# Two-block transformer kernel on one core: layer one's expert steps 256 to 512, with layer two's modulation moved into the first part of the routing, and its norm, queries and values set beside the last routing pass

## The chip, the cores and the metric

The kernel runs on one core of a Trainium2 chip. The metric is the device time of one execution, in microseconds (us), as the median of several runs. A core has TensorE (PE in the profile, with its weight loads as PEld), VectorE (DVE), ScalarE (ACT), GpSimd (POOL) and SyncE (SP). Here POOL only issues the gathers of expert rows, and SP only issues the loads of weights; both kinds of transfer run on the same 16 DMA engines.

## What is computed

Two different transformer blocks, one after the other, all in float32 on 256 tokens of width 1024. The first block has two layers and carries a context of another 256 tokens along, which layer two reads only for its keys and values. Each layer has a modulation (scales and shifts computed from a conditioning vector), attention with two softmax maps, two side branches, and a feed-forward part that is a memory of 16384 experts:

```python
for l in range(2):                                   # first block
    mod = (silu(c) @ w_mod[l] + b_mod[l]).reshape(b, 6, 1, d)   # 12 column blocks of 512
    xn = modulate(rms_norm(h, norm1_g[l]), mod[:, 0], mod[:, 1])
    p = xn @ w_in[l]                                 # queries, keys, values, pool, conv, gates
    q, k = rope(qk_heads(p[.., Q], q_norm_g[l])), rope(qk_heads(p[.., K], k_norm_g[l]))
    o = diff_attn(q, [k, k_context], [v, v_context])
    h = h + mod[:, 2] * mixer_output(o, p, ...)
    h = h + mod[:, 5] * peer_ffn(modulate(rms_norm(h, norm2_g[l]), ...), ...)
    # the context rows go through the same steps in layer one

def peer_ffn(x, w_q, sub_keys, u_emb, v_emb):        # per token
    s = scores of 8 heads x 2 halves against 128 sub-keys
    eidx, gate = top-16 of the sums of two top-16 lists, per head  # the "routing": 128 experts
    hid = gelu(x . u_emb[eidx])
    return sum_k(gate_k * hid_k * v_emb[eidx_k])
```

The second block (two layers of SwiGLU, retention, block attention and convolution) follows and is not touched.

## The kernel before

Tokens are held in blocks of 128, one token per partition. Layer one works on four of them: A0 and A1 (the sequence) and B2 and B3 (the context). The expert part of one block is 128 *steps*. In step s POOL gathers, for each of the 128 tokens, the row of its next expert (u and v side by side, 8 KB a token, so 1 MiB a gather); DVE multiplies the u half by the token and sums (L1717), ACT and DVE form the weight, ACT makes a diagonal matrix of it (L1131), and PE adds the v half into an accumulator through that diagonal (L698, two matmuls a row, printed as four; pairs of rows at a time, `V_LAG` = 3 steps behind). In blocks A1 and B3, which the code calls `SHARED`, PE does only one row in four this way, and DVE does the other three (L1710).

The steps of A0, A1, B2, B3 are numbered 0 to 511 and run without a break. Beside them each engine runs other work, written as generators that `yield` a number of *beats*; `weave(..., 2)` lets two beats of other work pass for each expert step. All three engines run the same sequence of yields (ACT and DVE two beats later than PE), so the place of every piece of other work in the steps is fixed by these numbers. From step 256 on the other work is `pe_ahead`, `act_ahead` and `dve_ahead`:

- the routing of B2's heads 2 to 7 in three passes of two heads, then that of B3 in one pass of eight heads (`pe_route_scores`, L674, and `dve_route_pass`). A pass of two heads has 46 yields which weigh 50 beats, times 0.62 by `scaled`; the pass of eight has 136 yields which weigh 161 beats, times 0.85;
- layer two's modulation (`pe_modulation`, L479 and L469): 12 column blocks, each with two weight tiles of 1 MiB. `together(a, b, rate)` gives one item of `a`, at no beats of its own, for `rate` yields of `b`;
- `pe_tokens`, times 0.8: layer two's first norm for the sequence (`pe_norm_turn`, L455), its queries (column blocks n = 0, 1), keys (2, 3) and values (4, 5) (`pe_qkv_heads`; L429, eight matmuls printed as sixteen for each n and block of tokens; `dve_qkv_heads` normalises the heads of queries and keys and rotates them), and then its mixer (`pe_mixer`: pool, conv and gate branches).

After step 511 comes the edge "hand over", where layer two goes on with the context's keys and values.

Weights come into a ring of four tiles of 1 MiB (`W`, slots of `wbuf`) in the order in which `sync` issues them; a tile is loaded as soon as the one that held its slot has been used, so the ring always holds the next four. Gathers go into a ring of ten slots (`gat`), from which `gat.held` leaves some out while their memory has another use: two of ten are left out up to gather 340 and three after it. A slot comes free when PE (or DVE) has used the v half of its row. The heads of queries and keys pass through the ring `side`, which lies in the memory that the routing also uses (`sc`), and partly in that of the routing's queries.

## Time and profile before

| | before |
|---|---|
| median of 3 runs | 4387.02 us (4383.78 to 4387.35) |
| profiled execution, its own time | 4379.6 us |
| its span, first to last instruction | 4377.8 us |
| PE / PEld busy | 3754.2 / 2394.2 us |
| DVE busy | 2843.8 us |
| ACT busy | 1153.1 us |
| DMA, mean over the span | 280 GB/s |

The rows come from one profiled execution. Busy time is a union per engine; the end of a matmul is modelled. "DMA share" in a stretch is the busy share of the 16 DMA engines. Arrows (`<-`) name what ended an idle time. The stretch in question runs from about 1509 us to 2371 us of the span.

### The profile page before, as it was taken

The numbers are of one execution on the slowest core, as the hardware profiler recorded it, in microseconds if no ns is written. First come the engines' busy times: TensorE is split into PE (matmuls) and PEld (weight loads), VectorE is DVE, ScalarE is ACT, GpSimd is POOL, SyncE is SP. The second block draws the span as 40 slices with busy tenths as digits, with TensorE's granted clock in tenths as the row PEclk, the third lists the DMA queues.
The fourth block names the chain that finished last, engine by engine and source line by source line (L and its number), as shares of the span: only waits on it lengthen the run. The fifth ranks groups of instructions, "written<-read, shape, count | busy, mean of one in ns | idle before, by whom it ended". The sixth has DMA issues, their size and how long they took to land. (4 is left out here: it accounts for less than half of the span.)

```text
span 4377.8 us, 42320 instructions
## 1 busy us (share of the span) xinstructions
PE 3754.2 (86%) x15261; PEld 2394.2 (55%) x15261; DVE 2843.8 (65%) x6607; ACT 1153.1 (26%) x2555; POOL 901.2 (21%) x772
## 2 busy tenths in 40 slices
PE   6989978788999787789896878777779989999898
PEld 3457444334746333245642544322229879998797
DVE  1441147988876777877877548886666576565765
ACT  2140011124011111131011411112114444444443
POOL 0000012433332333423332014544330000000000
PEclk7999989999999899999997989999999999999999
DMA  7114358987999999979996149999984534545343
GB/s 294 77 41 161 149 203 344 408 344 302 420 416 363 389 418 421 394 303 382 421 421 275 74 179 389 421 383 422 422 365 167 178 129 158 199 157 183 136 164 130
DMA packets 246622, 1225.90 MB, mean 280 GB/s; under 512 B 19256, under 2 KB 46202, under 8 KB 124428
## 3 DMA queue, kind: packets, MB, share of 16 engines
q0 software_dynamic: 110592, 805.36, 45.2%
q1 hardware_dynamic: 135820, 417.84, 25.5%
q8 instruction: 120, 1.97, 0.2%
q14 instruction: 90, 0.74, 0.0%
HBM read 1222.07 MB, written 1.05 MB: 279 GB/s over the span
## 5 line engine op out<-in xcount | busy, mean ns | idle before, releaser
L429 PE MATMUL ps<-wbuf,BIG 128*128 128x512 f32 x1856 | 812.0, 595 | 7.9 <-DMA wbuf<-in_t_conv_out_w 4.1
L2554 POOL DMA_INDIRECT gbuf<-in_t_uv,idx x286 | 336.5, 1176 | 1493.6 <-DVE BIG L1682 860.2
L429 PEld LDWEIGHTS ps<-wbuf,BIG 128*128 128x128 f32 x1856 | 352.0, 191 | 440.8 <-issue 431.6
L1758 DVE TENSOR_TENSOR plo<-wbuf,phi 128x1024 fp32r<-128x1024 f32 (+1 forms) x344 | 401.7, 1180 | 285.9 <-ACT phi L1166 285.2
L698 PE MATMUL ps<-gbuf,BIG 128*128 128x512 f32 x868 | 435.2, 641 | 150.9 <-ACT BIG L1131 144.3
L698 PE MATMUL ps<-BIG 128*128 128x512 f32 x904 | 438.8, 625 | 126.7 <-ACT BIG L1131 124.9
L1146 ACT ACTIVATE BIG<-BIG 128x2 f32<-128x2 f32 x384 | 78.1, 203 | 1480.1 <-DVE BIG L1724 1480.0
L1717 DVE CUSTOM_DVE_ANT_0 BIG<-BIG 128x1024 f32<-128x1024 f32 x292 | 355.9, 1222 | 156.2 <-DMA BIG<-in_t_uv,idx 155.2
L723 PE MATMUL ps<-XH,phi 128*128 128x256 f32 x1472 | 422.8, 287 | 24.9 <-DVE XL L1768 21.0
L2554 POOL DMA_INDIRECT BIG<-in_t_uv,idx x292 | 336.9, 1154 | 428.5 <-PE ps L698 362.7
L1717 DVE CUSTOM_DVE_ANT_0 gbuf<-gbuf,BIG 128x1024 f32<-128x1024 f32 x286 | 348.9, 1222 | 116.1 <-DMA gbuf<-in_t_uv,idx 115.2
L724 PE MATMUL ps<-XL,phi 128*128 128x256 f32 x1472 | 421.2, 286 | 0.0
L725 PE MATMUL ps<-XH,plo 128*128 128x256 f32 x1472 | 421.1, 286 | 0.0
L429 PE MATMUL ps<-BIG,wbuf 128*128 128x256 f32 x1920 | 420.4, 379 | 0.3 <-DMA wbuf<-in_t_conv 0.3
L1166 ACT CAST phi<-wbuf 128x1024 fp32r<-128x1024 f32 (+1 forms) x344 | 343.8, 1013 | 291.6 <-PE ps L725 291.0
L429 PEld LDWEIGHTS ps<-BIG,wbuf 128*128 128x128 f32 x1920 | 364.9, 190 | 63.4 <-issue 14.0
L698 PE MATMUL ps<-wbuf,BIG 128*128 128x512 f32 x604 | 312.2, 649 | 97.2 <-ACT BIG L1131 97.2
L698 PEld LDWEIGHTS ps<-BIG 128*128 128x128 f32 x904 | 173.7, 199 | 377.5 <-issue 197.5
L698 PEld LDWEIGHTS ps<-gbuf,BIG 128*128 128x128 f32 x868 | 166.3, 202 | 385.5 <-ACT BIG L1131 215.6
L2554 POOL DMA_INDIRECT wbuf<-in_t_uv,idx x190 | 227.6, 1198 | 432.2 <-PE ps L698 399.7
L723 PEld LDWEIGHTS ps<-XH,phi 128*128 128x128 f32 x1472 | 286.3, 194 | 26.8 <-DVE XL L1768 22.3
L1131 ACT ACTIVATE BIG<-ident,BIG 128x128 f32<-128x128 f32 x594 | 210.3, 395 | 296.9 <-DVE BIG L1700 279.5
(348 smaller groups left out, 5086.6 us busy)
## 6 DMA issues: line engine op xcount, KB each, us to landing
wbuf<-in_t_in SPq DMA_DIRECT2D x84, 1024.0 KB, 8.3
wbuf<-in_t_w_mod SPq DMA_DIRECT2D x48, 1024.0 KB, 9.3
wbuf<-in_ffn_wg SPq DMA_DIRECT2D x20, 2048.0 KB, 7.6
wbuf<-in_ffn_wu SPq DMA_DIRECT2D x20, 2048.0 KB, 7.7
wbuf<-in_t_conv SPq DMA_DIRECT2D x48, 768.0 KB, 8.6
wbuf<-in_ffn_wd SPq DMA_DIRECT2D x16, 2048.0 KB, 7.9
wbuf<-in_t_peer_wq SPq DMA_DIRECT2D x24, 1024.0 KB, 6.9
wbuf<-in_w_in SPq DMA_DIRECT2D x14, 1536.0 KB, 6.6
```

The costliest lines, as they stand in the source:

```text
L429: ins = p(mm)(bank, l, r, start=(k == 0), stop=(k == 7))
L698: ins = p(mm)(ps.of(("acc", T, tb, n)), dg, g[:, 1024 + n * 512:1536 + n * 512], start=(j == 0), stop=(j == last_on_pe(T, tb)))
L723: p(mm)(bank, lh, rh, start=(start and i == 0), stop=False)
L724: p(mm)(bank, lh, rl, start=False, stop=False)
L725: ins = p(mm)(bank, ll, rh, start=False, stop=(stop and i == n - 1))
L1131: a(act)(dg, ident[:, :], ACT.Copy, scale=wv[:, j:j + 1]).then_inc(act_exp.up(T, tb, "diag", j), 1)
L1146: a(act)(x2[:, j - 1:j + 1], x2[:, j - 1:j + 1], ACT.Tanh, scale=GELU_C * GELU_K).then_inc(act_exp.up(T, tb, "tanh", j // 2), 1)
L1166: a(copy)(piece_at(q)[0], W2.of(key, rows_, n)[:, k0:k1, c0:c1]).then_inc(act_piece.up(q), 1)
L1717: v(ttr)(row, row, XN[:, tb, :], 1.0, 0.0, ALU.mult, ALU.add, hid[:, j:j + 1]).then_inc(dve_exp.up(T, tb, "u", j), 1)
L1758: v(tt)(lo, W2.of(key, rows_, n)[:, k0:k1, c0:c1], hi.bitcast(F32), ALU.subtract).then_inc(dve_piece.up(q), 1)
L2554: g(nc.gpsimd.indirect_dma_start)(slot, None, I["t_uv"], bass.IndirectOffsetOnAxis(ap=idx[:, tb % 3, j:j + 1], axis=0)).then_inc(g_landed[ ...
```

## The change

In `*_ahead` of all three engines: the modulation is put beside the routing of B2's heads 2 to 7 alone, at one column block for 9 yields where it was 18. Then the one routing pass of B3 begins (one yield), and a new `alongside` sets the norm, the queries and the values (n = 0, 1, 4, 5) of layer two beside it: one beat of the tokens' work pulls 2.4 yields of the routing, and only the routing's beats count. Behind it come the keys (n = 2, 3) and the mixer as before, at 0.8. The heads go through a new ring `heads` (eight slots in the memory of the routing's queries) in place of `side`; ACT and DVE wait for the modulation before the norm; the third gather slot is left out from gather 300 and not 340; SP issues the weights in the new order.

```diff
+def alongside(a, b, rate):
+    m = 0
+    for n in a:
+        m += rate * (n or 1)
+        while m >= 1:
+            m -= 1
+            n = next(b, None)
+            if n is not None:
+                yield n
+    yield from b
...
+        heads = Ring([BIG[:, 8192 + i * 512:8704 + i * 512] for i in range(8)])
...
-        heads_ring = {"A": wide, "B": side, "C": side, "D": wide}
+        heads_ring = {"A": wide, "B": side, "C": heads, "D": wide}
...
         def pe_ahead(p):
             yield
-            routes = both(*(scaled(pe_route_scores(p, "B", "A", 2, h, h + 2), 0.62, 1) for h in (2, 4, 6)),
-                          scaled(pe_route_scores(p, "B", "A", 3), 0.85, 1))
-            yield from together(pe_modulation(p, 1), routes, 18)
-            yield from scaled(pe_tokens(p), 0.8, 1)
+            routes = both(*(scaled(pe_route_scores(p, "B", "A", 2, h, h + 2), 0.62, 1) for h in (2, 4, 6)))
+            yield from together(pe_modulation(p, 1), routes, 9)
+            routes = scaled(pe_route_scores(p, "B", "A", 3), 0.85, 1)
+            yield next(routes)
+            yield from alongside(pe_tokens(p), routes, 2.4)
+            yield from scaled(pe_keys(p), 0.8, 1)
...
             yield from pe_norm_turn(p, "C1", range(2))
-            yield from pe_qkv_heads(p, "C", "C1", 0, L, range(6), range(2))
+            yield from pe_qkv_heads(p, "C", "C1", 0, L, (0, 1, 4, 5), range(2))
+
+        def pe_keys(p):
+            L = second
+            yield from pe_qkv_heads(p, "C", "C1", 0, L, (2, 3), range(2))
             edge(p, ("attended", "C"))
             yield from pe_mixer(p, "C", 1, L)
...
         def act_tokens(a):
             L = second
             edge(a, "tokens")
+            a.wait_ge(*dve_mod.at(1, "A", 1))
...
         def dve_tokens(v):
             L = second
             edge(v, "tokens")
-            side.reset(*edges.events("tokens"))
+            v.wait_ge(*dve_mod.now())
+            heads.reset(*edges.events("tokens"))
...
-                if s == 340:
+                if s == 300:
                     gat.held = {7, 8, 9}
...
-            sync_qkv(s, "C", 1, 0, range(6))
+            sync_qkv(s, "C", 1, 0, (0, 1, 4, 5, 2, 3))
```

What it does to the order on the engines is seen at three places.

On PE, in the routing of B2's heads: the modulation's column blocks (L479 before, L493 after; `32x512 x8`) stand among the rows of the experts' v halves (L698 before, L712 after; two a row). Before, from the third block on:

```order
L479 MATMUL ps<-wbuf,BIG 32x512 x8
L469 MATMUL ps<-BIG 128x2 x4
L698 MATMUL ps<-gbuf,BIG 128x512 x2
L698 MATMUL ps<-wbuf,BIG 128x512 x2
L674 MATMUL ps<-BIG 128x128 x4
L698 MATMUL ps<-wbuf,BIG 128x512 x2
L698 MATMUL ps<-BIG 128x512 x6
L479 MATMUL ps<-wbuf,BIG 32x512 x8
```

After:

```order
L493 MATMUL ps<-wbuf,BIG 32x512 x8
L483 MATMUL ps<-BIG 128x2 x4
L712 MATMUL ps<-wbuf,BIG 128x512 x2
L712 MATMUL ps<-BIG 128x512 x6
L493 MATMUL ps<-wbuf,BIG 32x512 x8
L483 MATMUL ps<-BIG 128x2 x4
L712 MATMUL ps<-gbuf,BIG 128x512 x4
L493 MATMUL ps<-wbuf,BIG 32x512 x8
```

Between two column blocks there were six expert rows (twelve matmuls), and there are now two or four.

On PE, where the routing of B3 is done and layer two's norm (L455), first queries (L429) and their turn (L422) follow, before:

```order
L455 MATMUL ps<-BIG,H 128x128 x12
L429 MATMUL ps<-wbuf,BIG 128x512 x8
L698 MATMUL ps<-BIG 128x512 x2
L698 MATMUL ps<-gbuf,BIG 128x512 x6
L429 MATMUL ps<-wbuf,BIG 128x512 x8
L698 MATMUL ps<-wbuf,BIG 128x512 x4
L698 MATMUL ps<-BIG 128x512 x4
L429 MATMUL ps<-wbuf,BIG 128x512 x8
L422 MATMUL ps<-ident,sc 128x128 x4
```

After, the same work begins right behind B3's scores (L688; norm L469, queries L443):

```order
L688 MATMUL ps<-BIG 128x128 x16
L712 MATMUL ps<-wbuf,BIG 128x512 x2
L712 MATMUL ps<-BIG 128x512 x2
L469 MATMUL ps<-BIG,H 128x128 x4
...
L469 MATMUL ps<-BIG,H 128x128 x8
L712 MATMUL ps<-wbuf,BIG 128x512 x4
L443 MATMUL ps<-wbuf,BIG 128x512 x8
L712 MATMUL ps<-BIG 128x512 x4
L712 MATMUL ps<-gbuf,BIG 128x512 x6
L712 MATMUL ps<-wbuf,BIG 128x512 x4
L712 MATMUL ps<-BIG 128x512 x2
L443 MATMUL ps<-wbuf,BIG 128x512 x8
```

Between two blocks of queries there were four expert rows, and there are now eight.

On POOL, the gathers of one turn of the ring at about gather 310, before:

```order
L2554 DMA wbuf<-in_t_uv,idx 128x2048 x2
L2554 DMA BIG<-in_t_uv,idx 128x2048 x3
L2554 DMA gbuf<-in_t_uv,idx 128x2048 x3
```

After:

```order
L2588 DMA wbuf<-in_t_uv,idx 128x2048 x2
L2588 DMA BIG<-in_t_uv,idx 128x2048 x2
L2588 DMA gbuf<-in_t_uv,idx 128x2048 x3
```

One turn had eight slots there and has seven, as it had from gather 340 on before.

## Rows read from the trace of the kernel before

**Rows 1.** The page's part 2: the span in 40 slices of 109 us.
```profile
PEclk7999989999999899999997989999999999999999
DMA  7114358987999999979996149999984534545343
GB/s 294 77 41 161 149 203 344 408 344 302 420 416 363 389 418 421 394 303 382 421 421 275 74 179 389 421 383 422 422 365 167 178 129 158 199 157 183 136 164 130
```

**Rows 2.** Windows: stretch, length, busy us (xinstructions) by engine, clock, DMA share, GB/s.
```profile
1509.00:1663.60 154.60, 121.38 (x400) 51.73 (x401) 115.84 (x375) 27.44 (x85) 51.69 (x44) 0.89 0.98 405
1663.60:1775.00 111.40, 86.57 (x276) 37.92 (x275) 75.57 (x270) 20.10 (x63) 39.57 (x36) 0.91 1.01 421
1775.00:1869.30 94.30, 64.72 (x135) 24.95 (x133) 89.13 (x243) 16.78 (x56) 40.68 (x33) 0.96 0.97 381
1869.30:1882.00 12.70, 10.36 (x41) 6.92 (x42) 4.67 (x18) 4.75 (x10) 1.88 (x2) 0.73 0.55 189
1882.00:1934.00 52.00, 52.00 (x130) 23.44 (x129) 33.70 (x82) 17.54 (x36) 13.63 (x13) 1.00 0.79 304
1934.00:1983.00 49.00, 38.88 (x97) 17.78 (x96) 41.44 (x82) 18.59 (x32) 12.94 (x12) 0.90 0.82 329
1983.00:2050.00 67.00, 63.81 (x159) 28.60 (x157) 53.81 (x108) 12.35 (x30) 25.43 (x18) 1.00 0.98 390
2050.00:2313.00 263.00, 238.53 (x752) 145.25 (x753) 213.94 (x422) 26.63 (x85) 94.97 (x76) 0.97 1.01 418
2313.00:2371.00 58.00, 27.48 (x49) 10.11 (x48) 46.74 (x89) 3.90 (x14) 21.73 (x17) 0.75 0.99 403
```

**Rows 3.** DMA view of 1509 to 2371 us.
```profile
DMA packets 47939, 339.22 MB, mean 394 GB/s; under 512 B 5594, under 2 KB 5734, under 8 KB 8294
q0 software_dynamic: 36352, 264.70, 75.6%
q1 hardware_dynamic: 11548, 74.07, 20.9%
```

**Rows 4.** Timeline of PE: start us, us, instruction, count, idle before.
```profile
1508.89 3.46 PE L479 MATMUL ps<-wbuf,BIG 128*32 128x512 f32 x16 [6.41 <-DVE BIG L1306]
...
1653.32 1.92 PE L479 MATMUL ps<-wbuf,BIG 128*32 128x512 f32 x16
...
1663.61 3.73 PE L674 MATMUL ps<-BIG 128*128 128x128 f32 x32
...
1871.21 2.04 PE L455 MATMUL ps<-BIG,H 128*128 128x128 f32 x8 [3.42 <-DVE BIG L1358]
...
1881.95 7.03 PE L429 MATMUL ps<-wbuf,BIG 128*128 128x512 f32 x16
1888.82 1.88 PE L698 MATMUL ps<-BIG 128*128 128x512 f32 x4
...
1934.33 1.04 PE L422 MATMUL ps<-ident,modd 128*128 128x128 f32 x8
```

**Rows 5.** DMA view of 1676 to 1753 us: issues, median us to landing.
```profile
BIG<-in_t_uv,idx POOLq DMA_INDIRECT x11, 17.4
```

**Rows 6.** The same view, 1780 to 1862 us.
```profile
BIG<-in_t_uv,idx POOLq DMA_INDIRECT x8, 9.5
```

**Rows 7.** Timeline of DVE: the first block of queries.
```profile
1893.44 0.69 DVE L1433 TENSOR_REDUCE st<-sc 128x8 f32<-128x512 f32 x1 [5.42 <-ACT sc L982]
...
1894.89 0.20 DVE L1437 RECIPROCAL st<-st 128x8 f32<-128x8 f32 x1 [0.56 <-ACT st L925]
...
1898.19 0.69 DVE L1412 TENSOR_TENSOR sc<-sc,rope 128x512 f32<-128x512 f32 x1
...
1899.52 0.42 DVE L1417 TENSOR_TENSOR sc<-sc,BIG 128x256 f32<-128x256 f32 x1
```

**Rows 8.** Waits of DVE, 1869.3 to 1983 us: us in total, times, longest.
```profile
DVE st L1433 <- ACT sc L982: 12.2, 3, 5.6
DVE BIG L1358 <- PE ps L455: 6.9, 1, 6.9
```

More of the change, by code:

```diff
@@ L2396, in act_tokens, with act_keys @@
             edge(a, "tokens")
+            a.wait_ge(*dve_mod.at(1, "A", 1))
             yield from act_norm_turn(a, "C1", L, range(2), colA(1, 0), colB(1, 0))
-            yield from act_qkv_heads(a, "C", "C1", 1, 0, L, range(6), range(2), side)
+            yield from act_qkv_heads(a, "C", "C1", 1, 0, L, (0, 1, 4, 5), range(2), heads)
+        def act_keys(a):
+            L = second
+            yield from act_qkv_heads(a, "C", "C1", 1, 0, L, (2, 3), range(2), heads)
             edge(a, ("attended", "C"))
@@ L2515, in dve_tokens, with dve_keys @@
             edge(v, "tokens")
-            side.reset(*edges.events("tokens"))
+            v.wait_ge(*dve_mod.now())
+            heads.reset(*edges.events("tokens"))
             yield from dve_norm_turn(v, "C1", L, range(2), colA(1, 0), colB(1, 0), "A experts", sideb)
-            yield from dve_qkv_heads(v, "C", "C1", 1, 0, L, range(6), range(2), side)
+            yield from dve_qkv_heads(v, "C", "C1", 1, 0, L, (0, 1, 4, 5), range(2), heads)
+        def dve_keys(v):
+            L = second
+            yield from dve_qkv_heads(v, "C", "C1", 1, 0, L, (2, 3), range(2), heads)
             edge(v, ("attended", "C"))
@@ L2708, in restart @@
             last.clear()
-            for ring in (ps, gat, diag, mrows, big, tmp, wide, side, side4, narrow, sideb, sts):
+            for ring in (ps, gat, diag, mrows, big, tmp, wide, side, side4, heads, narrow, sideb, sts):
                 ring.reset()
```

20 lines of the change are left out of this document (12 added, 8 removed).

## Prediction

> **What bounds the kernel now.** I read first the page's slices. From the seventh to the twenty-first the DMA line is near full [rows 1]: while experts run, transfers set the pace, and the stretch that the change touches (slices 14 to 22) runs at 382 to 421 GB/s with one dip, to 303, in the eighteenth slice, before it ends in the last of them. Second, I cut this stretch by its content. Markers on PE give the cuts [rows 4]: the modulation's first column block at 1508.9 us, its eighth at 1653.3; B3's scores (L674 x32) at 1663.6; the norm at 1871.2; the first queries at 1882.0; the turn of the gate columns (L422 on modd) at 1934.3, which stands at the border from B2's rows to B3's. The code's yields agree: three passes at 31 beats are 46.5 steps, and the window from 1509.0 to 1663.6 us has 44 gathers; 161 times 0.85 beats are 68.5 steps, and the next two windows have 69 [rows 2].
>
> Third, the price of a byte. At 421 GB/s one MiB takes 2.49 us. The first window moved 405 GB/s times 154.6 us, which is 59.7 MiB: its 44 gathers and 16 weight tiles. So time there is bytes. Over the whole stretch the two queues moved 339 MB, which is three quarters gathers [rows 3], and the change moves the same bytes. What it can win is only the time in which the DMA engines were short of work. I take it per window as its length times (1 - GB/s / 421) [rows 2]: 5.9 us to 1663.6; 0 and 9.0 us in B3's routing; 7.0 in the norm; 14.5 to 1934; 10.7 to 1983; 4.9 to 2050; 1.9 to 2313; 2.5 at the end. Together 56 us, of which 32 lie between 1869 and 1983 us.
>
> Why there? From 1882 to 1934 PE is busy 52.00 of 52.00 us. A block of queries or keys takes PE 7.03 us and an expert row up to 1.88 us [rows 4]; the plan puts 3.2 steps between two blocks, so a turn costs 7 + 3.2 times 1.8, about 13 us, while its 4.2 MiB need 10.5 us. That is a stretch bound by PE. In the 94.3 us before, DVE is busy 89.13 us [rows 2]: the second half of the routing is bound by DVE. And in the window before that one neither is full (DVE 75.57 and PE 86.57 of 111.4 us), because weights fill the DMA engines. The change puts PE's work from the third kind of place beside DVE's work of the other two.
>
> **Part one, modulation beside B2's heads 2 to 7.** At 9 yields a block, 138 yields take all twelve blocks. In the window the ring then loads 24 tiles and not 16: 8 MiB more, +19.9 us. DVE needs 115.84 us and PE 121.38 us (at a granted clock of 0.89) of some 174 us, and eight gather slots are still there up to gather 300, with landings of 17.4 us at worst when weights compete [rows 5]; one turn of that ring would be 8 times 3.9 us. So I add no wait: between 0 and +5 us (waits of PE for a weight tile, which this stretch does not show at L479), taken as 0.
>
> **Part two, norm, queries and values beside B3's routing.** This stretch took 205.7 us for 79 MiB. Its tiles are still eight (the last four of modulation and the first of the queries before; values and keys after), so its floor by bytes stays 205.7 - 9.0 = 196.7 us. DVE had 164.7 us of work. Four blocks of queries add 4.6 us each: five operations of 0.69 us, for which L1433 and L1412 stand, two of 0.42 and two small ones [rows 7]; the norm adds at most the 4.67 us of its window. That makes 188 us. PE has 69 rows at up to 1.88, eight blocks at 6.9 (1881.95 to 1888.82), B3's scores at 3.7 and the norm at under 5, at most 194 us. So three engines stand at 96 to 98% of 197 us at once. Something gives way. Two places show how far it goes. In 1775 to 1869, with seven slots, DVE reached 94.5% and DMA 0.97; in 1983 to 2050 PE reached 95% with DMA at 0.98. DVE's 188 us at 94.5% are 199 us. On top come its waits in its own order: the heads wait for ACT's square, which waits behind PE's block, and the second diagonal of the norm waits for PE [rows 8]. Half of the 12.2 us (four of eight blocks) and the norm's 6.9 us make 13, of which I take 12, since the blocks stand eight steps apart. 211 us, +5.3 us. The bounds: 197 (nothing collides) and 232 (a wait of 5.6 us, the longest seen, at each of four blocks, and 6.9 us for the norm: 188 + 29 = 217, at 94.5%: 230, rounded up for the slots).
>
> The seventh slot goes 40 gathers earlier. With seven slots the rows landed in 9.5 to 9.7 us [rows 6] and the stretch ran at 94.3 / 33 = 2.86 us a row; I need 211 / 69 = 3.06, so the slots alone don't bind. Behind DVE's waiting instruction stand the next rows' products, behind them ACT's diagonals and PE's v halves, and for these POOL waits: this is how a collision would reach the DMA engines.
>
> **Part three, what lies behind.** From 1869.3 to 2371 it was 501.7 us. Eight tiles fewer are loaded: -19.9 us. Of the 41.5 us of short DMA the norm's 7.0 go; four key blocks remain beside B2's last 13 steps at the same spacing, so four fifths of 14.5, 11.6; at the border to B3 (10.7 us) blocks of heads are replaced by the mixer's first blocks, which ask nothing of DVE: half of it, 5; of the 4.9 behind it, 2, since the values are gone; 1.9 stays. The other work now ends at step 477 (371 and half of 211 beats, keys and mixer) and not at 498 (371 and half of 254, with norm, queries and values). The end is left with bare gathers, where DVE with three v halves of four has 46.74 us of work for 17 rows, 2.75 us each with what is left of the mixer, more than DMA's 2.49. I charge 21 more steps with 0.15 us: 2.5 becomes 5.5. Losses 26 in place of 41.5: -15.5 us (between -5, if the border stays as bad and the keys lose as much as all five blocks did, and -21).
>
> The edits that cost nothing: ACT's and DVE's waits for the modulation (it ends 12 yields of routing before the pass does, about four steps; without that cover, one step); the ring `heads` (same number of slots; its memory is free once B3's scores are computed, and these stand ahead of the norm on PE). B3's indices are ready at step 371 as before, seven steps ahead of their first gather.
>
> **Sum.** +19.9 + 5.3 - 19.9 - 15.5 = -10.2 us. The profiled execution took 4379.6 us in all (span 4377.8), so its like would take 4369.4. The median of the runs shown is 4387.0, 7.4 above; on it the forecast is 4376.8 us. What follows after the hand over is the same work.
>
> **A rule against a row.** The windows show 421 GB/s held for 111 us [rows 2]. The Trainium skill, Perfetto Trace Analysis, Engine Utilization, gives 358 GB/s as a core's peak from HBM; by it 79 MiB could not pass in less than 231 us, and part two alone would cost 25 us. The row decides against the figure. The same page, Identifying the Most-Contended Engine, says that a kernel whose busiest engine changes from regime to regime may gain from interleaving them. The trace bears out that there are such regimes here.
>
> **The rivals.**
> - *Full overlap.* The engines' slack meets perfectly: part two takes 202 us. It would need DVE at 93% and all bursts of 7 us hidden behind the gathers in flight. For it: 2050 to 2313 holds 418 GB/s with PE at 91% and DVE at 81%; against it: there only one row in four passes through PE, so slots come free without it. -19 us, 4368. The interleaving rule would give this.
> - *The gain is eaten.* Waits are moved, not removed: part two takes 217 to 226 us, as the norm and every block of queries meet rows that all need PE. For it: each place with unshared rows and blocks of this kind in the trace lost a fifth (0.79, 0.82). 4387, between 4383 and 4392.
> - *Three engines in a lock, slower.* DVE waits at each query block for PE as long as it did at worst (5.6 us), and seven slots leave too little in flight: part two takes 232 us, +26 on its own. It decides above 221 us there (+15.5). Total +10.8, 4398. Against it: eight steps between blocks give PE time to catch up.
>
> **How the numbers follow.** 0.2% (8.8 us) is about what a measurement of this kernel can tell from no change. The forecast's case (4371 to 4382) 0.36, of which 0.28 is beyond 0.2%; full overlap 0.12; the gain eaten 0.28; the lock 0.24. Faster 0.40, same 0.36, slower 0.24. The range from 4361 to 4403 leaves out the farthest fifth: full overlap without any border loss, and a lock that also holds up the keys.
>
> **What would show it.** In the new profile the last modulation block stands at about 1680 us, the window to it at 420 GB/s; B3's routing ends at about 1895 us, with DVE over 88% in it and DMA near 0.95; the low windows of 0.55 and 0.79 are gone but for one of some 40 us; the hand over comes at about 2365 us and not 2375. I am wrong if B3's routing takes over 221 us, if DVE's waits for ACT's squares pass 15 us there, or if the DMA engines are short in the first window.

## The result, and the profile after

The changed kernel takes 4399.70 us (median of 6 runs, 4396.67 to 4403.48), the kernel before beside it on the same chip 4384.14 us (6 runs, 4381.15 to 4387.35): 1.004 times as long, interval 1.003 to 1.005, so 15.6 us slower, where 10 us less were forecast. The profiled execution of the changed kernel took 4400.78 us, with a span of 4399.0 us.

The GB/s in the page's slices of the kernel after, to be held against [rows 1]; slices 14 to 22 hold the stretch in question:

```profile
GB/s 293 77 43 159 149 203 354 407 345 295 420 412 363 384 421 350 358 363 386 420 421 287 77 148 389 421 389 417 421 383 166 177 127 161 197 156 181 135 163 129
```

The dip of the eighteenth slice (303 GB/s before) is gone, and in its place four slices stand at 350 to 386. The timeline of PE gives the cuts (start us, us, instruction, count, idle before), as in [rows 4]:

```profile
1692.44 3.73 PE L688 MATMUL ps<-BIG 128*128 128x128 f32 x32
...
1705.70 2.05 PE L469 MATMUL ps<-BIG,H 128*128 128x128 f32 x8 [6.09 <-DVE BIG L1372]
...
1724.54 7.03 PE L443 MATMUL ps<-wbuf,BIG 128*128 128x512 f32 x16
```

The scores of B3 now stand at 1692.4 us, the last reciprocal of B3's routing on DVE at 1921.0 (1867.6 before), and the hand over from B2's rows to the next ones, which [rows 4] marks by the turn of the gate columns at 1934.3 us, at 1985.5. The second such turn, at the end of the stretch, is at 2394.2 us (2375.4 before). The windows by content:

```profile
1514.00:1692.40 178.40, 143.54 (x504) 62.31 (x505) 116.80 (x378) 29.47 (x89) 47.92 (x44) 0.86 0.99 406
1692.40:1725.00 32.60, 24.33 (x99) 14.74 (x98) 23.09 (x81) 12.21 (x31) 9.34 (x9) 0.90 0.74 269
1725.00:1775.00 50.00, 44.61 (x100) 18.87 (x99) 37.86 (x130) 13.10 (x30) 16.87 (x17) 0.97 0.92 369
1775.00:1834.00 59.00, 50.35 (x110) 21.43 (x109) 50.09 (x159) 15.53 (x37) 17.11 (x18) 0.88 0.91 365
1834.00:1884.00 50.00, 50.00 (x124) 22.57 (x123) 37.33 (x121) 9.68 (x28) 13.60 (x13) 1.00 0.86 332
1884.00:1921.50 37.50, 29.32 (x59) 11.93 (x58) 33.60 (x68) 6.37 (x21) 16.13 (x14) 0.91 0.99 401
1921.50:1985.00 63.50, 61.73 (x156) 28.00 (x155) 42.54 (x102) 21.96 (x42) 15.43 (x15) 1.00 0.84 327
1985.00:2013.00 28.00, 26.45 (x70) 12.30 (x69) 19.96 (x36) 5.71 (x16) 6.73 (x8) 1.00 0.84 323
2013.00:2282.00 269.00, 241.53 (x757) 145.68 (x756) 218.02 (x432) 26.32 (x86) 105.69 (x82) 0.96 1.01 421
2282.00:2390.00 108.00, 41.90 (x60) 14.65 (x60) 93.75 (x184) 7.96 (x29) 42.69 (x35) 0.70 0.99 399
```

From marker to marker (first block of the modulation, B3's scores, last reciprocal of B3's routing, second turn of the gate columns):

| stretch | before | after | difference | forecast |
|---|---|---|---|---|
| modulation beside B2's heads | 154.7 | 178.5 | +23.8 | +19.9 |
| B3's routing | 204.0 | 228.6 | +24.6 | +5.3 |
| from there to the second turn | 507.8 | 473.2 | -34.6 | -35.4 |

The three make +13.8 us. The two profiled executions differ by 21.2 us: 5.1 more lie ahead of 1514 us and 2.3 behind 2394, where the program is the same, and single executions of the changed kernel spread over 6.8 us. The medians differ by 15.6. So the third stretch gave what was forecast, the first cost 4 us more, and most of the miss is in B3's routing: 19.3 of the 24.0 us between the forecast's -10.2 and the +13.8 measured.

Lost DMA time, worked out as in the prediction (length times 1 minus GB/s over 421), says where: 11.8 us in the norm's 32.6 us, 6.2 and 7.8 in the two windows of the queries, 10.6 in the values' 50 us, 1.8 behind. That is 38 us, where the forecast of 211 us allowed 14. The waits of this stretch (1692.4 to 1921.5 us) are, in us in total, times and longest, first DVE's:

```profile
DVE BIG L1731 <- DMA BIG<-in_t_uv,idx: 16.7, 7, 6.3
DVE gbuf L1731 <- DMA gbuf<-in_t_uv,idx: 15.4, 9, 6.9
DVE wbuf L1731 <- DMA wbuf<-in_t_uv,idx: 4.0, 3, 3.0
DVE st L1451 <- ACT st L939: 1.7, 4, 0.6
DVE st L1366 <- ACT st L939: 1.6, 1, 1.6
DVE st L1447 <- ACT BIG L996: 0.6, 1, 0.6
```

and POOL's, which issues the gathers:

```profile
POOL gbuf L2588 <- PE ps L712: 70.5, 28, 8.1
POOL BIG L2588 <- PE ps L712: 51.5, 20, 9.4
POOL wbuf L2588 <- PE ps L712: 31.4, 18, 7.4
```

DVE hardly waits for ACT's squares (0.6 us at L1447 in place of the 12.2 of [rows 8]); it waits 36 us for gathers. Before, it waited about as long for them (34.2 us), but then with the DMA engines at 403 GB/s over the stretch; now they stand at 351, since POOL waits for slots: 153.4 us against 122.2 before. What POOL waits for is the v half of a row on PE (L712). The timelines side by side show the same pattern at each of the eight blocks, here at the second and third of the values. PE:

```profile
1848.53 7.03 PE L443 MATMUL ps<-wbuf,BIG 128*128 128x512 f32 x16
1855.40 0.60 PE L436 MATMUL ps<-ident,BIG 128*128 128x128 f32 x4
1855.84 3.60 PE L712 MATMUL ps<-gbuf,BIG 128*128 128x512 f32 x8
1859.27 3.60 PE L712 MATMUL ps<-wbuf,BIG 128*128 128x512 f32 x8
1862.71 7.03 PE L443 MATMUL ps<-wbuf,BIG 128*128 128x512 f32 x16
```

POOL:

```profile
1848.97 0.94 POOL L2588 DMA_INDIRECT gbuf<-in_t_uv,idx  x1 [0.78 <-PE ps L712]
1857.99 0.94 POOL L2588 DMA_INDIRECT gbuf<-in_t_uv,idx  x1 [8.09 <-PE ps L712]
1859.71 0.94 POOL L2588 DMA_INDIRECT gbuf<-in_t_uv,idx  x1 [0.78 <-PE ps L712]
...
1871.73 0.98 POOL L2588 DMA_INDIRECT BIG<-in_t_uv,idx  x1 [7.65 <-PE ps L712]
```

A block of 16 matmuls holds PE for 7.03 us; no v half ends in that time, no slot comes free, and POOL issues nothing for 8 us. Then four rows follow each other at 1.72 us and the next block begins. The norm shows a second form of it: PE stands 6.09 us for the first diagonal (L469 at 1705.70, above) with rows queued behind, and POOL waits 9.4 us.

All eight pauses of POOL at a block are 7.4 to 8.1 us long, but they did not all cost the same. The windows from one block to the next, four of queries and four of values:

```profile
1724.50:1746.00 21.50, 20.90 (x49) 9.04 (x48) 14.15 (x52) 5.87 (x13) 7.49 (x8) 1.00 0.77 290
1746.00:1773.70 27.70, 22.91 (x50) 9.46 (x49) 22.91 (x77) 7.03 (x17) 8.53 (x8) 0.94 1.01 423
1773.70:1795.20 21.50, 21.28 (x53) 9.43 (x52) 18.52 (x67) 6.43 (x17) 8.10 (x8) 1.00 0.83 320
1795.20:1834.40 39.20, 30.76 (x62) 12.75 (x61) 33.16 (x101) 9.30 (x22) 9.88 (x10) 0.83 0.95 391
1834.40:1848.50 14.10, 14.10 (x37) 6.44 (x36) 11.58 (x37) 3.19 (x9) 4.41 (x4) 1.00 0.60 213
1848.50:1862.70 14.20, 14.20 (x37) 6.47 (x36) 10.14 (x32) 2.86 (x8) 3.75 (x4) 1.00 0.98 377
1862.70:1876.40 13.70, 13.70 (x33) 6.08 (x32) 8.07 (x26) 2.07 (x7) 4.51 (x4) 1.00 0.92 370
1876.40:1890.20 13.80, 13.80 (x34) 6.11 (x33) 13.20 (x35) 2.46 (x8) 4.23 (x4) 1.00 0.96 386
```

They lost 6.7, 0, 5.2 and 2.8 us of DMA time, then 7.0, 1.5, 1.7 and 1.1. The three that lost most follow another pause of POOL closely (9.4 and 4.2 us at the norm, 6.7 us before the third block of queries, 7.0 and 6.3 us before the first of values). Ahead of the second and the fourth block of queries POOL had issued eight gathers some 1.7 us apart, faster than the DMA engines take them (2.49 us), and enough was on its way to last through the pause (423 GB/s in the second window). The last three blocks of values lose what a turn bound by PE loses: four rows and a block take it 14 us, their transfers 12.5. So a pause costs by what is on its way when it begins. No experiment below sets two pauses apart to test this reading by itself.

### The profile page after: what moved, and what is told of

The parts are those of the page before. It is cut to its first block and busy times, and to the rows that moved or that the text cites. A ratio compares the mean times of both kernels' runs of the same rounds, so it can differ in the third digit from the quotient of the medians.

```text
span 4399.0 us, 42317 instructions
## 1 busy us (share of the span) xinstructions
PE 3770.2 (86%) x15261; PEld 2403.3 (55%) x15261; DVE 2842.0 (65%) x6607; ACT 1153.4 (26%) x2555; POOL 875.9 (20%) x772
## 5 line engine op out<-in xcount | busy, mean ns | idle before, releaser
L443 PE MATMUL ps<-wbuf,BIG 128*128 128x512 f32 x1856 | 816.7, 597 | 6.2 <-issue 2.2
L712 PE MATMUL ps<-gbuf,BIG 128*128 128x512 f32 x884 | 455.9, 657 | 164.9 <-ACT BIG L1145 159.9
L443 PEld LDWEIGHTS ps<-wbuf,BIG 128*128 128x128 f32 x1856 | 353.6, 192 | 442.0 <-issue 433.9
L712 PE MATMUL ps<-BIG 128*128 128x512 f32 x888 | 432.1, 627 | 129.4 <-ACT BIG L1145 129.3
L443 PE MATMUL ps<-BIG,wbuf 128*128 128x256 f32 x1920 | 421.5, 380 | 0.3 <-DMA wbuf<-in_t_conv 0.3
L2588 POOL DMA_INDIRECT BIG<-in_t_uv,idx x288 | 324.8, 1128 | 436.2 <-PE ps L712 370.1
L443 PEld LDWEIGHTS ps<-BIG,wbuf 128*128 128x128 f32 x1920 | 365.6, 191 | 63.5 <-issue 14.0
L712 PEld LDWEIGHTS ps<-gbuf,BIG 128*128 128x128 f32 x884 | 175.0, 207 | 412.0 <-ACT BIG L1145 227.7
L712 PEld LDWEIGHTS ps<-BIG 128*128 128x128 f32 x888 | 170.0, 199 | 373.6 <-issue 187.9
L712 PE MATMUL ps<-wbuf,BIG 128*128 128x512 f32 x604 | 301.6, 631 | 74.4 <-ACT BIG L1145 74.3
L1731 DVE CUSTOM_DVE_ANT_0 wbuf<-wbuf,BIG 128x1024 f32<-128x1024 f32 x192 | 234.4, 1222 | 96.9 <-DMA wbuf<-in_t_uv,idx 96.6
## 6 DMA issues: line engine op xcount, KB each, us to landing
wbuf<-in_t_w_mod SPq DMA_DIRECT2D x48, 1024.0 KB, 10.4
```

The source lines that it names most:

```text
L443: ins = p(mm)(bank, l, r, start=(k == 0), stop=(k == 7))
L712: ins = p(mm)(ps.of(("acc", T, tb, n)), dg, g[:, 1024 + n * 512:1536 + n * 512], start=(j == 0), stop=(j == last_on_pe(T, tb)))
L1731: v(ttr)(row, row, XN[:, tb, :], 1.0, 0.0, ALU.mult, ALU.add, hid[:, j:j + 1]).then_inc(dve_exp.up(T, tb, "u", j), 1)
L2588: g(nc.gpsimd.indirect_dma_start)(slot, None, I["t_uv"], bass.IndirectOffsetOnAxis(ap=idx[:, tb % 3, j:j + 1], axis=0)).then_inc(g_landed[ ...
```

## The experiments

Each total stands with its ratio to the kernel before, run beside it on the same chip, and the 95% interval of that ratio; the changed kernel itself is at 1.004 (1.003 to 1.005). The lengths of stretches come from one profiled execution each. How far they can be trusted shows in the modulation's stretch: its program is the same in the changed kernel and in twelve of the variants, and it took between 178.2 and 182.8 us. A difference of 4 to 6 us in one stretch is therefore near what single executions differ by, and one of 11 or more is clear of it.

The first four were set against three theories. **R**: the 7 us blocks hold back the v halves, and a ring of seven slots runs dry. **D**: DVE is the bound, by the work of the heads. **S**: the seventh slot given up 40 gathers earlier is the cost by itself. The column "B3" below is always the stretch from B3's scores on PE to the last reciprocal of its routing on DVE; "rest" goes on to the second turn of the gate columns.

**e1, the slot alone.** In the kernel before:

```diff
-                if s == 340:
+                if s == 300:
                     gat.held = {7, 8, 9}
```

> The kernel before with one edit: the third gather slot is left out from gather 300 and not 340. The changed kernel took 229 us from B3's scores on PE to the last operation of B3's routing on DVE, where the kernel before took 204. Theory S (the slot alone): seven slots carry too little in flight, and this kernel loses 15 us or more in that stretch and in all. Theory R (blocks on PE against the ring): seven slots are short only where PE's blocks of 7 us hold back the v halves, and there are none here; it loses 0 to 4 us. Theory D (DVE bound by the heads' work): no change.

Measured: 4381.74 us, 0.9993 of before (0.9983 to 1.0002); B3 203.4 us. S is out: without blocks of queries and values on PE the ring of seven is enough. It is enough even though POOL pauses as long here, up to 9.6 us, where PE waits for the next diagonals:

```profile
1776.85 0.95 POOL L2554 DMA_INDIRECT wbuf<-in_t_uv,idx  x1 [9.58 <-PE ps L698]
```

```profile
1767.00:1777.00 10.00, 4.20 (x5) 1.85 (x6) 6.75 (x26) 1.10 (x4) 0.42 (x2) 0.69 1.02 427
```

The DMA engines stayed full through the pause; SP had issued four weight tiles between 1729.9 and 1755.1 us.

**e2, the modulation alone.** In the kernel before (norm, queries and values stay behind B3's routing, and the eighth slot stays up to gather 340), with the same edit for ACT and DVE:

```diff
-            routes = both(*(scaled(pe_route_scores(p, "B", "A", 2, h, h + 2), 0.62, 1) for h in (2, 4, 6)),
-                          scaled(pe_route_scores(p, "B", "A", 3), 0.85, 1))
-            yield from together(pe_modulation(p, 1), routes, 18)
+            routes = both(*(scaled(pe_route_scores(p, "B", "A", 2, h, h + 2), 0.62, 1) for h in (2, 4, 6)))
+            last_route = scaled(pe_route_scores(p, "B", "A", 3), 0.85, 1)
+            yield from together(pe_modulation(p, 1), routes, 9)
+            yield from last_route
             yield from scaled(pe_tokens(p), 0.8, 1)
```

> The kernel before with the modulation alone moved: at 9 yields a block beside B2's heads 2 to 7, then B3's routing with nothing beside it, then norm, queries, keys, values and mixer as before. By bytes the stretch to B3's scores takes 20 to 24 us longer, as in the changed kernel (178.5 after 154.7), and the 8 MiB come back later. B3's routing has 69 MiB and 165 us of DVE's work, so by theories R and D alike it takes 174 to 182 us in place of 204. In all 0 to 8 us faster than before. If the loss of the change lies in the modulation's move, this kernel is slower than before by 10 us or more.

Measured: 4383.18 us, 0.9998 (0.9988 to 1.0007); modulation 178.2 us, B3 178.7, rest 509.8. What the modulation takes earlier it gives back in B3's routing, to within 2 us. All of the loss belongs to what runs beside B3.

**e3, less of PE.** After, with one matmul of eight in the blocks of layer two's queries and values; seven eighths of these products are left out:

```diff
-                    gemm8(p, b, key, 512, lambda k, w: (xt(L, k, tb), w)).then_inc(pe_qkv.up(T, n, tb), 1)
+                    gemm8(p, b, key, 512, lambda k, w: (xt(L, k, tb), w),
+                          (7,) if T == "C" and n in (0, 1, 4, 5) else range(8)).then_inc(pe_qkv.up(T, n, tb), 1)
```

> The changed kernel, but each block of layer two's queries and values for the sequence is one matmul and not eight (seven of eight terms of the sum are left out; weights are loaded and waited for as before, DVE and ACT do all their work). That takes 8 times 6 us of work from PE, in bursts of 7 us. Theory R: the ring runs free, the stretch from B3's scores to the end of its routing falls from 229 to 210 us or less, in all 19 us or more faster than the changed kernel (4381 or less). Theory D: DVE still has 188 us of work and its own waits; the stretch stays above 220 us.

Measured: 4383.9 us, 1.0001 (0.9991 to 1.0011); B3 212.7 us, 15.9 less. The window of this stretch:

```profile
1688.20:1901.00 212.80, 157.38 (x372) 69.45 (x371) 180.56 (x547) 56.30 (x146) 78.95 (x69) 0.90 0.95 376
```

PE's busy time is 41 us less than the 198.6 of after, DVE's is the same, and the lost DMA time is 22.7 us in place of 38. In the total the whole excess over the kernel before goes with PE's blocks, in the stretch 15.9 of its 24.6 us. R's bounds (210 us, 4381) were missed by 3 us each, and D, which put the stretch above 220, is contradicted. This run takes away PE's work and the length of its pieces at once; which of the two matters it can't tell.

**e4, less of DVE.** After, without the rotation of layer two's queries and with their gain on one column of 64 only (the rest is left out of the result); of the edit:

```diff
+                    bare = T == "C" and n < 2
...
-                    if tb < 2:
+                    if tb < 2 and not bare:
                         s2 = ring.claim(v, ("rot", T, n, tb), (pe_qkv, (T, n, tb, "turn")))
```

> The changed kernel, but DVE leaves out most of the work on the heads of layer two's queries for the sequence (the gain on 63 of 64 columns, and the rotation): 2.9 us of work less at each of four blocks, 12 us in all, inside the stretch of B3's routing. Theory D: the stretch falls from 229 by 12 us or more. Theory R: DVE has slack there, it falls by 0 to 4 us, and so does the total against the changed kernel (4396 to 4400).

Measured: 4400.17 us, 1.0036 (1.0023 to 1.0048); B3 228.1 us:

```profile
1692.80:1921.10 228.30, 198.31 (x485) 90.16 (x484) 170.14 (x528) 56.52 (x146) 73.99 (x69) 0.93 0.88 350
```

DVE has 11.8 us less to do, and the stretch takes as long. D is out.

The next four take the mechanism of R by its two handles, the length of a block and the depth of the ring, and leave all the work in.

**e5, blocks in halves.** After, with the call of `gemm8` written out as a loop, and

```diff
+                    for k in range(8):
+                        if k == 4 and T == "C":
+                            yield 2
...
-                    yield 4
+                    yield 2 if T == "C" else 4
```

> After, with every block of layer two's norm-fed queries, keys and values on PE cut in two halves of four matmuls (3.5 us each in place of 7.03 us), two beats of routing between the halves and two behind them in place of four behind the block: the same work, in smaller pieces. Theory R (a block of 7 us keeps PE from the v halves of the rows already landed, so the gather slots come back late and the ring of seven runs dry): the pauses of POOL behind a block shrink from about 8 us to 4 to 5, and B3's routing with the blocks in it goes from 228.6 us to between 213 and 221; total 4385 to 4393 us. Theory W (the time goes with the sum of PE's and DVE's work and not with the length of a piece): 226 to 231 us, no change of the total. The norm's part (some 12 us lost in its first 33 us) stays in either.

Measured: 4393.23 us, 1.0028 (1.0018 to 1.0038); B3 224.4 us, 4.2 less: below what W allows and short of what R expected, and by its total not to be told from after. POOL's pauses at the half blocks did shrink, to between 3.3 and 5.9 us. The long ones that are left (8.1 us at the norm, 9.2 and 10.4 us ahead of 1773 and 1823 us) are those in which PE waits for ACT's diagonals or for the norm. A smaller block helps, but alone only a little.

**e6, an eighth slot.** After, with the lines below; ACT's waits for the slot's memory move to match.

```diff
+                if s == 316:
+                    left["first 7"] = left[7]
+                    gat.held, gat.freed[7] = {8, 9}, ((pe_norm, ("C1", 1, 1)),)
+                if s == 420:
+                    gat.held = {7, 8, 9}
```

> After, with an eighth gather slot from gather 316 to gather 420, where after has seven (its memory is free once PE has read the second diagonal of the norm, and is claimed again ahead of the mixer's gates). Nothing else changes. Theory R: the eighth slot holds 3 us more of transfers in flight while PE is in a block, so each of the eight blocks loses up to 3 us less: B3's routing goes from 228.6 to between 212 and 221 us, total 4384 to 4392 us. Theory W (the engines' work, not the depth of the ring): 226 to 231 us. Since the eighth slot comes back only behind the norm, the norm's own loss of some 12 us stays.

Measured: 4386.3 us, 1.0012 (1.0001 to 1.0024); B3 222.9 us, 5.7 less, rest 466.5, 6.7 less than after. The stretch lies between what R (212 to 221) and W (226 to 231) expected; the total is clear of after's and within R's 4384 to 4392.

**e7, blocks in halves in the kernel before.** The edit of e5 there.

> The kernel before with the same cut of layer two's blocks into halves; there all of them stand behind B3's routing, from 1882 us on, beside B2's last rows. Theory R: the windows 1882 to 1934 and 1934 to 1983 us lost 14.5 and 10.7 us of DMA time because each block stopped the v halves for 7 us; with halves they lose a third to a half less, so the total is 4 to 10 us shorter than before, 4374 to 4380 us. Theory P (PE is simply full there, 52.00 of 52.00 us, whatever the order): no change, within 2 us.

Measured: 4380.33 us, 0.9993 (0.9981 to 1.0005); no change that can be told. The 52 us that followed the norm, PE busy 52.00 of 52.00 and 304 GB/s in [rows 2], read thus:

```profile
1878.00:1930.00 52.00, 52.00 (x135) 23.87 (x134) 31.27 (x76) 17.34 (x34) 15.13 (x14) 1.00 0.80 307
```

P holds there, and R's 4 to 10 us do not come: with PE full, halving its pieces changed nothing.

**e8, halves and eighth slot.** Both edits on after.

> After with both edits: blocks cut in halves, and the eighth slot from gather 316 to 420. Theory R: the stretch goes to between 206 and 213 us (its floor by bytes is 197, and some 10 us of the norm's loss stay), total 4377 to 4385 us, no slower than the kernel before. If the two edits act on the same loss, their sum falls short: 210 to 216 us. Theory W: 226 to 231 us.

Measured: 4385.6 us, 1.0004 (0.9993 to 1.0014); B3 213.4 us, 15.2 less, 0.4 above R's range and within that of "the same loss"; the total is 0.6 above R's. In the stretch the two together come out above their sum (4.2 and 5.7). In the totals they do not: by the ratios e5 alone is worth some 5 us, e6 alone 12 and both 16. The window:

```profile
1692.50:1906.40 213.90, 190.41 (x485) 87.59 (x484) 179.58 (x546) 56.10 (x146) 82.17 (x70) 0.96 0.94 375
```

With PE's and DVE's work all in, the stretch is as short as e3's, which left out most of the blocks' matmuls. This speaks against W and for R. Where each edit helps is seen when the lost DMA time is worked out by part of the stretch, from the same cuts on PE in each trace (first block of queries, first of values, 14 us behind the start of the last block of values):

| lost DMA time, us | norm | four blocks of queries | four of values | behind |
|---|---|---|---|---|
| after | 11.4 | 14.6 | 11.3 | 0.6 |
| e5, halves | 11.4 | 9.1 | 12.9 | 0.2 |
| e6, eighth slot | 11.6 | 6.9 | 11.4 | 0.1 |
| e8, both | 10.8 | 3.2 | 9.4 | 0.0 |
| e10, and the norm's head earlier | 6.5 | 3.7 | 9.6 | 0.0 |

Both edits work on the queries, and there their gains (5.5, 7.7, together 11.4) do not exceed their sum. The values hardly gain: PE is full there, 55.80 of 55.80 us in after and in e6, and stays so.

```profile
1825.80:1881.60 55.80, 55.80 (x138) 25.09 (x137) 43.98 (x130) 10.58 (x31) 18.15 (x16) 1.00 0.88 335
```

**e9, the norm's head earlier.** On after, DVE's sum and first diagonal and ACT's root ahead of B3's first piece (`begun` runs a generator up to its first yield); for DVE, and likewise for ACT:

```diff
+            tokens = begun(dve_tokens(v))
             yield next(routes)
-            yield from alongside(dve_tokens(v), routes, 2.4)
+            yield from alongside(tokens, routes, 2.4)
```

> After, with the head of the norm (DVE's sum and mean of the squares, ACT's wait for the modulation and its root, DVE's reciprocal and first diagonal) placed ahead of DVE's and ACT's first piece of B3's routing, where after has it behind; PE's order is the same. In after PE stands at the norm from 1699.6 to 1705.7 us for that diagonal, with two rows' v halves behind it, POOL waits 9.4 us for their slots, and the first 33 us of the stretch lose 11.8 us of DMA time. Theory N (that wait is the norm's loss): PE's wait of 6.1 us is gone, the first 33 us lose 3 to 7 us, the stretch goes from 228.6 to between 219 and 225 us, total 4390 to 4396 us. Theory M (the loss there comes from the routing's own start, its scores on PE and unshared rows of POOL, and the diagonal only fills the time): 226 to 231 us.

Measured: B3 223.8 us, 4.8 less; the total 4400.24 us, 1.0029 (1.0018 to 1.0041), is not told from after's by its interval. The first window:

```profile
1697.30:1730.30 33.00, 27.93 (x108) 16.59 (x107) 27.39 (x98) 12.99 (x34) 12.02 (x9) 0.95 0.85 309
```

It loses 8.8 us and not 11.8; PE's wait for the first diagonal is 1.8 us in place of 6.09. The wait was a part of the norm's loss, the smaller one. N's place is right and its stretch (219 to 225) held, but more was left than the 3 to 7 us it allowed, and its total (4390 to 4396) did not come. Part of the gain is hidden in the profiled execution, which reached the first block of the modulation 3.8 us later than after's, ahead of anything that this edit changes.

**e10, all three.** After with halves, eighth slot and earlier head.

> After with all three edits: blocks of queries, keys and values cut in halves, the eighth slot from gather 316 to 420, and the head of the norm ahead of the routing's first piece. The first two together gave 213.4 us in the stretch and 4385.6 us in all. Theory N: 204 to 209 us there, total 4376 to 4382 us, that is 0.1 to 0.2% faster than the kernel before. Theory M: 211 to 216 us, total 4383 to 4388 us.

Measured: 4380.84 us (11 runs) against 4384.62 (17 runs), 0.9989 (0.9980 to 0.9998), so 4 us less than the kernel before and hardly clear of the noise; B3 210.7 us, 2.7 less than e8, between the two theories, and the total within N's. Of its windows:

```profile
1694.20:1727.20 33.00, 29.66 (x113) 17.52 (x112) 27.46 (x98) 12.99 (x34) 13.91 (x10) 0.95 0.87 318
1727.20:1777.20 50.00, 48.24 (x116) 21.30 (x115) 43.91 (x147) 14.87 (x35) 20.80 (x20) 1.00 1.00 404
1777.20:1836.20 59.00, 52.51 (x124) 23.11 (x123) 53.98 (x169) 16.24 (x39) 22.63 (x20) 0.97 1.00 407
```

The queries' windows are now at 404 and 407 GB/s, where after had 369 and 365, with the same blocks in them.

**e11, the norm alone beside B3; e12, norm and values.** After, with the other blocks behind the routing. Of the edit of e12, which is made on ACT, DVE and SP too:

```diff
-            yield from pe_qkv_heads(p, "C", "C1", 0, L, (0, 1, 4, 5), range(2))
+            yield from pe_qkv_heads(p, "C", "C1", 0, L, (4, 5), range(2))
...
-            yield from pe_qkv_heads(p, "C", "C1", 0, L, (2, 3), range(2))
+            yield from pe_qkv_heads(p, "C", "C1", 0, L, (0, 1, 2, 3), range(2))
```

> After with only the norm beside B3's routing: all twelve blocks of queries, keys and values stand behind it, in the order of the kernel before. With the modulation alone moved the stretch took 178.7 us. Theory R+N (the stretch of 228.6 us is these 178.7, some 20 us for the bytes of eight tiles, some 12 for the norm, and about 18 for eight blocks, 2.2 us each): 187 to 193 us here, and total 4383 to 4390 us. Theory T (the loss comes only when norm, blocks and routing meet and DMA is already behind): the norm alone costs under 5 us, 179 to 184 us, total 4380 to 4384 us.

> After with the norm and the four blocks of values beside B3's routing, and the eight blocks of queries and keys behind it. Theory R+N: 178.7 + 12 (norm) + 10 (four tiles) + 9 (four blocks at 2.2 us) = 210, between 205 and 214 us, total 4386 to 4395 us. Theory T: most of the loss needs the queries, whose blocks DVE follows with 4.6 us each: 198 to 204 us, total 4380 to 4386 us.

Measured, e11: 4391.72 us, 1.0011 (1.0000 to 1.0021), 1.7 above R+N's range; B3 189.9 us, rest 503.5. Against e2 the norm costs 11.2 us in the routing and gives back 6.3 behind it. e12: 4405.33 us, 1.0043 (1.0026 to 1.0061); B3 205.3 us, so four blocks of values cost 15.4 more, 10 of it their four tiles. From there to after, with four blocks of queries and four tiles more, it is 23.3. R+N held for both stretches, T for neither; but by equal blocks R+N would have put queries no dearer than values (5.4 against 13.3 us beyond the bytes). e12's total missed both, since its rest is 506.0 us, with four blocks fewer than e11's 503.5. PE's timeline has most of the reason, at the hand over:

```profile
1995.25 3.49 PE L712 MATMUL ps<-BIG 128*128 128x512 f32 x4 [11.67 <-ACT BIG L1145]
1998.58 0.60 PE L436 MATMUL ps<-ident,BIG 128*128 128x128 f32 x4
2009.76 1.09 PE L436 MATMUL ps<-ident,BIG 128*128 128x128 f32 x4 [10.58 <-DVE BIG L1432]
```

The first wait is in e11 too (11.0 us), the second is not: PE comes to the turn of a head that DVE, in its own order behind its rows, rotates only at 2009.2 us. In this order of the blocks that head comes too late for PE's place.

**e13, the values spaced.** In the code a block of queries is followed by 8 beats and one of values by 4; in after's trace the queries stand 21.5 to 27.7 us apart and the values 14. On after, for PE, ACT and DVE:

```diff
                     if n >= 4:
+                        if T == "C":
+                            yield 3
                         continue
```

> After with three beats more behind each of layer two's four blocks of values (on PE, ACT and DVE alike), so that they stand some 24 us apart and not 14, and reach into the last 37 us of the stretch, which hold no block in after. Nothing else changes. Theory Q (four rows and a block take PE 14 us and DMA only 12.5, so the values' 49 us are a stretch bound by PE, which lost 10.2 us of DMA time): the stretch goes from 228.6 to between 219 and 225 us, total 4390 to 4396 us. Theory R alone (each block of 7 us costs its pause of POOL wherever it stands): 226 to 231 us, no change of the total.

Measured: B3 223.1 us, 5.5 less; the total 4396.99 us, 1.0037 (1.0022 to 1.0051), is after's within the interval, as R said. The stretch lies in Q's range, but not for Q's reason:

```profile
1687.40:1910.50 223.10, 191.49 (x465) 85.94 (x464) 181.60 (x552) 56.17 (x146) 74.81 (x68) 0.92 0.89 351
```

At the 351 GB/s of after it moved 2.0 MiB less, which is 5.0 us, and its lost DMA time is 37.1 us against 38.1. The fourth block of values had slipped out: it begins at 1910.5 us, where the stretch ends, and the rest takes 480.7 us, 7.5 more. The other values stand 17.6 and 31.2 us apart, and the window behind the first of them still loses 7.5 us. So this run doesn't show that spacing the values recovers DMA time.

**e14, all four edits.** The edits of e10 and e13 on after.

> After with all edits: blocks in halves, the eighth slot, the head of the norm ahead of the routing's first piece, and the values spaced. With the first three the stretch took 210.9 us and the kernel 4380.8 us. Theory Q: 204 to 209 us, total 4373 to 4379 us. Theory R alone: 209 to 213 us, total 4379 to 4383 us.

Measured: 4378.41 us (12 runs) against 4381.70 (17 runs), 0.9991 (0.9982 to 1.0000). B3 204.3 us, at Q's lower end and as long as before the change, though it holds the norm, the queries and three of the four blocks of values; the fourth begins 2.8 us before its end. Against e10 it loses 4 us less of DMA time (15.5 and 19.5) and moves 1.0 MiB less, and the rest takes 476.7 us, 4.9 more. In all it is e10 within the intervals.

## Why the prediction was wrong, by its own steps

**The failed step is part two**, "211 us, +5.3 us". It priced the collision on the channel of DVE's own waits (12 us for ACT's squares and the second diagonal) and took DVE at 94.5% as the limit. DVE's waits for ACT came to 4 us, DVE was busy 182 of 229 us, and taking 11.8 us of its work away changed nothing (e4). In its place the runs showed the ring: a block of 7.03 us stops the v halves, POOL waits up to 8 us for a slot, and DMA runs at 332 to 369 GB/s with no engine's average near its bound except PE's in the values' window. The sum allowed 14 us of lost DMA time in part two and 38 were measured: 11.4 at the norm, 14.6 at the queries, where the edits of the ring and of the blocks' length took 11.4 back (e8), and 11.3 at the values, where PE is full and they took 2.

The text had this path in its last sentence ("this is how a collision would reach the DMA engines") and then ruled it out two lines above: "the slots alone don't bind", from 2.86 us a row with seven slots. That rate was read where PE's longest piece was a row of 1.88 us. It was a mean, and what was needed was a depth. An estimate of it from rows: seven slots are worth 7 times 2.49 us, 17.4 us; a gather takes 9.5 us to land [rows 6], which leaves 8 us for DVE, ACT, the v half and any pause. A pause of 8 us uses all of it. This holds for gathers alone and for a ring that is full when the pause begins: in e1 a pause of 9.6 us behind weight tiles cost nothing, and in after the pauses that came soon after another one cost 5 to 7 us, others next to nothing. e1 shows that the seven slots cost nothing without blocks; e6 and e8 that with blocks the eighth makes the stretch 5.7 us shorter, and 11.0 once the blocks are halved.

Some sums of part two were off by less: DVE's 188 us are 95% of 197 and not 96; 221 us in part two is +15.3 and not +15.5. Neither moves the result.

**"The blocks stand eight steps apart"** was wrong for the values, which stand four rows apart. There four rows and a block take PE 14 us and DMA 12.5 (four rows and a tile), so the values brought along the PE-bound place that [rows 2] shows at 1882 us: PE 50.00 of 50.00 us, 332 GB/s. Its price is 9 to 13 us of DMA time in after, e5, e6, e8 and e10 alike. Whether spacing would save it is not shown: e13 and e14 do not keep all four blocks in the stretch.

**The norm** was given 6.9 us of DVE's waiting; it cost 11.2 in the routing (e11) and gave back 6.3 and not 7.0 behind. DVE's wait for PE is gone from the list of waits; PE's for the first diagonal took its place and was a part of the cost, some 3 to 4 us of it (e9, e10).

**Part one** was right in kind and 4 us too small. The window moved 406 GB/s times 178.4 us, 69.1 MiB, 9.4 more than before and not 8; its lost DMA time is 6.4 us as against 5.9. The 1.4 MiB too many are missing in the next stretch, which moved 76.7 MiB and not 79, so for the sum this is nothing. e2 confirms it: moved alone, the modulation is neutral (4383.18 us against 4384.90). That PE and ACT would not wait held but for a few us (PE 3.0 for tiles, 3.2 for ACT).

**Part three was right**: -34.6 us against -35.4. The windows behind 1921.5 us lose 14.2, 6.5, 0 and 5.6 us, 26.3 together; the forecast had 26.

**The rivals.** The measured total is where "three engines in a lock" put it (4398), and its point of decision, 221 us in part two, is borne out: 228.6 was over it, and e8 and e10, at 213 and 211, come out level with the kernel before. That e6 does so nearly (1.0012) at 222.9 it owes to its shorter rest. Half of its mechanism held, "seven slots leave too little in flight"; the other half, DVE waiting 5.6 us at each block of queries, did not (0.6 us in all). What it had against itself, "eight steps between blocks give PE time to catch up", asked the wrong question: PE catches up, but the slots it held back are late by then. That its 232 us for part two lies 3 us from the 228.6 measured is in part luck, since it was added up from those waits of DVE. Full overlap was the far case; e14 comes to 204.3 us in the stretch, near its 202, with a block of values moved behind it, and pays part of it back there.

Two rules of the Trainium skill were weighed in the prediction. The windows of the kernel after hold 421 GB/s for 269 us (2013 to 2282). The Trainium skill, Perfetto Trace Analysis, Engine Utilization, gives 358 GB/s, but for a core whose neighbour in the pair uses the memory too; for a core alone the same section names some 435 GB/s of its 16 DMA engines as the bound and about 120% of 358 as the practical ceiling. The prediction left this out, and its 231 us for 79 MiB is not what the section would give for a kernel on one core; the measured 421, which is 118% of 358, agrees with it.

Interleaving stretches with different bounds made the kernel 15.6 us slower as written; with halved blocks, an eighth slot and the norm's head earlier it was 0.1% faster (e10), at the edge of the noise. The Trainium skill, Perfetto Trace Analysis, Optimization Strategy (the prediction names the section before it), says that performance may be improved by interleaving such regimes. These runs agree with no more than that "may".

**What stays open.** Why adding the queries (after against e12) costs 13.3 us beyond their bytes and adding the values (e12 against e11) 5.4. In after itself the two lose 14.6 and 11.3 us of DMA time, so between them the gap is 3 us and not 8; where the rest comes from is open, and e4 rules out only the gain and the rotation on DVE. Whether halving and the eighth slot help each other is not shown: the stretch says so by 5 us, the totals do not. Of the norm's loss 7 to 8 us remain in e10; after the first wait was gone, the second diagonal still held PE for 2.9 us, and the rest was not followed.

## What to carry to other kernels

Where a ring of buffers hides the latency of transfers, weigh a burst put on an in-order engine against the depth of the ring in time (slots times the pace, less the landing), not against the engine's mean load: PE at 87% and DVE at 79% can stand beside DMA engines at 351 of 421 GB/s. Look at what comes just before the burst, too: the pauses that cost were those that met a ring already thinned. Before interleaving, cut the burst and see whether a slot can be had; and look at every spacing in the plan, as two kinds of blocks may not have the same, and where the engine is simply full neither remedy helps (e7, and the values in e5 and e6). And when a stretch gets shorter, count what is in it and follow what is freed to the end: e13's stretch was 5 us shorter because a block and 2 MiB had left it, and e12, with four blocks fewer behind its routing than e11, took longer there.

## What the runs showed of the hardware

Nothing of the chip itself was unexpected. How well a single stretch repeats depends on the stretch: B3's routing took 204.0, 203.4 and 203.7 us in before, e1 and e7, and 228.6 and 228.1 in after and e4, but the modulation's stretch, the same program in after and twelve variants, took 178.2 to 182.8 us. Totals of single runs of one kernel spread over up to 19 us.
